# Building the gate matrix: the gating moved from GpSimd to ScalarE and VectorE, the loops written out

## The reference, cut to what matters

```python
best, ci = lax.top_k(cand, PEER_TOPK)
i1 = jnp.take_along_axis(top_i[..., 0, :], ci // PEER_TOPK, axis=-1)
i2 = jnp.take_along_axis(top_i[..., 1, :], ci % PEER_TOPK, axis=-1)
idx = i1 * PEER_N_KEYS + i2
g = jax.nn.softmax(best, axis=-1)
...
act = jax.nn.gelu(jnp.einsum('ckd,cd->ck', u_tab[ic], xc), approximate=False)
return jnp.einsum('ck,ckd->cd', (gc * act).astype(v_tab.dtype), v_tab[ic])
```

## Time and profile before

| | us |
|---|---|
| median of three timed runs | 2910.61 |
| lowest, highest of them | 2907.49, 2912.16 |
| the profiled execution's own time | 2909.95 |
| its span, first to last instruction | 2908.2 |
| VectorE busy | 2039.8 (70%) |
| TensorE matmul busy | 2516.1 (87%) |
| ScalarE busy | 1022.2 (35%) |
| GpSimd busy | 675.6 (23%) |

### The profile page before, as it was taken

One profiled execution on the slowest core, in us unless ns is written; L12 is line 12 of the kernel. 1 busy time (PEld: TensorE's weight loads), 2 busy tenths in 40 slices (PEclk: granted clock), 3 DMA queues, 4 the chain that ended last, 5 costly groups with the idle time before them and its releaser, 6 DMA issues. The chain is left out here.

```text
span 2908.2 us, 44667 instructions
## 1 busy us (share of the span) xinstructions
PE 2516.1 (87%) x15526; PEld 2263.0 (78%) x15528; DVE 2039.8 (70%) x3316; ACT 1022.2 (35%) x1576; POOL 675.6 (23%) x548
## 2 busy tenths in 40 slices
PE   7979267999999999888791679999999998768898
PEld 6758156999999999777581569999999997758797
DVE  7667999666666666586679996666666665649652
ACT  4321023444444444433210234444444443434321
POOL 5580265000000000046703650000000000616340
PEclk9879678999999999987796889999999999879898
DMA  5434000555555555453430015555555554324201
GB/s 191 145 116 147 20 0 29 189 187 188 188 187 188 187 186 186 133 182 130 135 133 8 0 42 189 188 188 187 188 187 186 185 186 144 117 102 145 66 1 37
DMA packets 107648, 392.09 MB, mean 135 GB/s; under 512 B 11952, under 2 KB 13360, under 8 KB 107184
## 3 DMA queue, kind: packets, MB, share of 16 engines
q1 hardware_dynamic: 107568, 391.02, 40.4%
HBM read 389.93 MB, written 1.05 MB: 134 GB/s over the span
## 5 line engine op out<-in xcount | busy, mean ns | idle before, releaser
L578 PEld LDWEIGHTS bank<-x_parts,chunk_parts 128*128 128x128 f32 x6144 | 770.5, 191 | 23.1 <-DVE chunk_parts L1126 3.5
L578 PE MATMUL bank<-x_parts,chunk_parts 128*128 128x256 f32 x6144 | 776.9, 283 | 2.5 <-DVE chunk_parts L1126 2.5
L1126 DVE TENSOR_TENSOR chunk_parts<-weight_ring,chunk_parts 128x1024 fp32r<-128x1024 f32 x512 | 625.3, 1222 | 195.6 <-ACT chunk_parts L762 195.6
L590 PE MATMUL bank<-chunk_parts,weight_parts 128*128 128x512 f32 x3072 | 744.8, 391 | 0.5 <-DVE chunk_parts L1126 0.5
L762 ACT CAST chunk_parts<-weight_ring 128x1024 fp32r<-128x1024 f32 x512 | 535.5, 1047 | 359.6 <-PE bank L590 359.6
L590 PEld LDWEIGHTS bank<-chunk_parts,weight_parts 128*128 128x128 f32 x3072 | 560.7, 188 | 106.8 <-issue 0.9
L1118 DVE TENSOR_TENSOR work<-work,big 128x256 f32<-128x256 f32 x256 | 162.9, 636 | 277.3 <-ACT work L766 277.3
L1094 DVE TENSOR_TENSOR weight_ring<-constants,work 128x512 f32<-128x512 f32 x256 | 262.3, 1100 | 4.1 <-ACT work L748 4.1
L766 ACT ACTIVATE work<-bank 128x256 f32<-128x256 f32 x256 | 98.3, 384 | 465.2 <-PE bank L578 465.2
L555 PE MATMUL bank<-weight_ring 128*128 128x128 f32 x1024 | 183.0, 335 | 83.9 <-issue 74.9
L555 PEld LDWEIGHTS bank<-weight_ring 128*128 128x128 f32 x1024 | 159.6, 238 | 107.7 <-issue 99.1
(11 more groups left out here) (355 smaller groups left out, 2788.7 us busy)
## 6 DMA issues: line engine op xcount, KB each, us to landing
weight_ring<-in_experts SPq DMA_DIRECT2D x512, 512.0 KB, 3.3
big<-in_ada SPq DMA_DIRECT2D x48, 512.0 KB, 4.0
weight_ring<-in_w_in SPq DMA_DIRECT2D x40, 512.0 KB, 4.6
weight_ring<-in_wq SPq DMA_DIRECT2D x32, 512.0 KB, 3.2
weight_ring<-in_gdn_in SPq DMA_DIRECT2D x32, 512.0 KB, 3.4
weight_ring<-in_w_out SPq DMA_DIRECT2D x16, 640.0 KB, 4.2
weight_ring<-in_lru_in SPq DMA_DIRECT2D x16, 512.0 KB, 3.3
weight_ring<-in_w_kv SPq DMA_DIRECT2D x8, 512.0 KB, 4.5
```

Of the source, the lines that this page charges most:

```text
L578: last = nc.tensor.matmul(nc_ps[2 + n % 2][:, 0:T], a[:, j * P:(j + 1) * P], xr[:, x, j], start=(j == 0 and a is hi and x == 0), stop=(j = ...
L590: last = nc.tensor.matmul(nc_ps[4 + 2 * tt + c][:, 0:512], wr[:, x, n % 2, tt * P:(tt + 1) * P], v[:, c * 512:(c + 1) * 512], start=False, ...
L1126: nc.vector.tensor_tensor(split[:, k % SPLITS, 1], wring[:, (N_ALL + k) % WSLOTS, 0:D], split[:, k % SPLITS, 0].bitcast(F32), ALU.subtract ...
```

## The change: what it does

- GpSimd's `gate_rows` and its loop are gone. GpSimd has nothing to do in the stage.
- VectorE compares only three of the four first one-hots (128 x 384, `first_hot`). The fourth it makes gated, in one instruction with two pointer scalars: equal to the key, then times the gate (128 x 128). The second one-hots stay as they were.
- ScalarE multiplies the three others by their gates, in place, with three 128 x 128 activations (Copy with a scale that is read from `slot`), one group ahead of its copy of the bank: the order on ScalarE is gate group g+1, copy group g.
- `ha` and `hb` are both rings of three groups (HOTS = 3), the PSUM banks stay two (G_BANKS = 2).
- On TensorE, ScalarE and VectorE the 64 groups are written out, with constant counts in place of registers; the semaphores start at zero.

```diff
+HOTS = 3
+ACT_GATED = 3
+G_BANKS = 2
...
-    ha = hot(4, 4, P)
-    hb = hot(2, 4, P)
+    ha = hot(HOTS, 4, P)
+    hb = hot(HOTS, 4, P)
...
-                        sp.wait_ge(s("g_ready"), 4 + GROUPS)
+                        sp.wait_ge(s("g_ready"), GROUPS)
...
-                def gate_products(g, count):
-                    pe.wait_ge(s("first_gated"), count)
-                    pe.wait_ge(s("second_hot"), count)
-                    pe.wait_ge(s("g_kept"), count)
+                for g in range(GROUPS):
+                    pe.wait_ge(s("first_gated"), g + 1)
+                    pe.wait_ge(s("second_hot"), g + 1)
+                    if g == 0:
+                        pe.wait_ge(s("slots_kept"), 1)
+                    if g >= G_BANKS:
+                        pe.wait_ge(s("g_kept"), g - G_BANKS + 1)
                     for j in range(4):
-                        last = nc.tensor.matmul(nc_ps[g % 2][:, j * P:(j + 1) * P], ha[:, g % 4, j], hb[:, g % 2, j], start=True, stop=True)
+                        last = nc.tensor.matmul(nc_ps[g % G_BANKS][:, j * P:(j + 1) * P], ha[:, g % HOTS, j], hb[:, g % HOTS, j], start=True, stop=True)
                     last.then_inc(s("g_ready"), 1)
-                with pe.Fori(0, GROUPS // ROUND) as i:
-                    for g in range(ROUND):
-                        gate_products(g, i * ROUND + (g + 1))
...
-                with act.Fori(0, T // 8) as i:
-                    for g in range(2):
-                        act.wait_ge(s("g_ready"), i * 2 + (g + 5))
-                        nc.scalar.copy(G[:, bass.ds(i * 8 + 4 * g, 4)], nc_ps[g][:, :].rearrange("p (a c) -> p a c", a=4)).then_inc(s("g_kept"), 1)
+                def gate_rows(g):
+                    act.wait_ge(s("first_hot"), g + 1)
+                    for j in range(ACT_GATED):
+                        last = nc.scalar.activation(ha[:, g % HOTS, j], ha[:, g % HOTS, j], ACT.Copy, scale=slot[:, 2, 4 * g + j:4 * g + j + 1])
+                    last.then_inc(s("first_gated"), 1)
+                gate_rows(0)
+                for g in range(GROUPS):
+                    if g + 1 < GROUPS:
+                        gate_rows(g + 1)
+                    act.wait_ge(s("g_ready"), g + 1)
+                    nc.scalar.copy(G[:, 4 * g:4 * g + 4], nc_ps[g % G_BANKS][:, :].rearrange("p (a c) -> p a c", a=4)).then_inc(s("g_kept"), 1)
...
-                def gate_rows(g, position, count):
-                    pool.wait_ge(s("first_hot"), count)
-                    nc.gpsimd.tensor_tensor(ha[:, g % 4], ha[:, g % 4], slot[:, 2, bass.ds(position, 4)].unsqueeze(2).broadcast_to([P, 4, P]),
-                                            ALU.mult).then_inc(s("first_gated"), 1)
...
-                def one_hot(out, half, position, ready):
-                    nc.vector.tensor_tensor(out, iota.unsqueeze(1).broadcast_to([P, 4, P]),
-                                            slot[:, half, bass.ds(position, 4)].unsqueeze(2).broadcast_to([P, 4, P]),
-                                            ALU.is_equal).then_inc(s(ready), 1)
...
+                def first_hot(g):
+                    if g >= HOTS:
+                        dve.wait_ge(s("g_ready"), g - HOTS + 1)
+                    n = ACT_GATED
+                    nc.vector.tensor_tensor(ha[:, g % HOTS, 0:n], iota.unsqueeze(1).broadcast_to([P, n, P]),
+                                            slot[:, 0, 4 * g:4 * g + n].unsqueeze(2).broadcast_to([P, n, P]), ALU.is_equal).then_inc(s("first_hot"), 1)
+                    for t in range(4 * g + n, 4 * g + 4):
+                        nc.vector.tensor_scalar(ha[:, g % HOTS, t % 4], iota, slot[:, 0, t:t + 1], slot[:, 2, t:t + 1], ALU.is_equal, ALU.mult)
+                first_hot(0)
+                for g in range(GROUPS):
                     if g + 1 < GROUPS:
-                        dve.wait_ge(s("g_ready"), g + 2)
-                        one_hot(ha[:, (g + 1) % 4], 0, 4 * (g + 1), "first_hot")
-                    dve.wait_ge(s("g_ready"), g + 3)
-                    one_hot(hb[:, g % 2], 1, 4 * g, "second_hot")
-                dve.wait_ge(s("g_kept"), 2 + T // 4)
+                        first_hot(g + 1)
+                    if g >= HOTS:
+                        dve.wait_ge(s("g_ready"), g - HOTS + 1)
+                    nc.vector.tensor_tensor(hb[:, g % HOTS], iota.unsqueeze(1).broadcast_to([P, 4, P]), slot[:, 1, 4 * g:4 * g + 4].unsqueeze(2).broadcast_to([P, 4, P]),
+                                            ALU.is_equal).then_inc(s("second_hot"), 1)
+                dve.wait_ge(s("g_kept"), GROUPS)
```

More of the change, by code:

```diff
@@ L223, in first_block @@
     hot.at = WSIZE + D
-    ha = hot(4, 4, P)
-    hb = hot(2, 4, P)
+    ha = hot(HOTS, 4, P)
+    hb = hot(HOTS, 4, P)
     GROUPS = T // 4
-    ROUND = 4
     out_e = big[:, 0:D]
@@ L546, in _ @@
                     last.then_inc(s("slots_turned"), 1)
-                def gate_products(g, count):
-                    pe.wait_ge(s("first_gated"), count)
-                    pe.wait_ge(s("second_hot"), count)
-                    pe.wait_ge(s("g_kept"), count)
+                for g in range(GROUPS):
[5 more added lines that the diff above has]
+                        pe.wait_ge(s("g_kept"), g - G_BANKS + 1)
                     for j in range(4):
-                        last = nc.tensor.matmul(nc_ps[g % 2][:, j * P:(j + 1) * P], ha[:, g % 4, j], hb[:, g % 2, j], start=True, stop=True)
+                        last = nc.tensor.matmul(nc_ps[g % G_BANKS][:, j * P:(j + 1) * P], ha[:, g % HOTS, j], hb[:, g % HOTS, j], start=True, stop=True)
                     last.then_inc(s("g_ready"), 1)
-                with pe.Fori(0, GROUPS // ROUND) as i:
-                    for g in range(ROUND):
-                        gate_products(g, i * ROUND + (g + 1))
-                pe.wait_ge(s("g_kept"), 2 + T // 4)
+                pe.wait_ge(s("g_kept"), GROUPS)
                 pe.wait_ge(s("zeros"), 1)
@@ L750, in _ @@
                 act.wait_ge(s("slots_kept"), 1)
-                act.sem_inc(s("g_kept"), 2)
-                with act.Fori(0, T // 8) as i:
-                    for g in range(2):
-                        act.wait_ge(s("g_ready"), i * 2 + (g + 5))
-                        nc.scalar.copy(G[:, bass.ds(i * 8 + 4 * g, 4)], nc_ps[g][:, :].rearrange("p (a c) -> p a c", a=4)).then_inc(s("g_kept"), 1)
+                def gate_rows(g):
[9 more added lines that the diff above has]
+                    nc.scalar.copy(G[:, 4 * g:4 * g + 4], nc_ps[g % G_BANKS][:, :].rearrange("p (a c) -> p a c", a=4)).then_inc(s("g_kept"), 1)
                 def high(k, slot_, loaded, free):
@@ L843, in _ @@
                                             ALU.mult).then_inc(s("hit_keyed"), 1)
-                def gate_rows(g, position, count):
-                    pool.wait_ge(s("first_hot"), count)
-                    nc.gpsimd.tensor_tensor(ha[:, g % 4], ha[:, g % 4], slot[:, 2, bass.ds(position, 4)].unsqueeze(2).broadcast_to([P, 4, P]),
-                                            ALU.mult).then_inc(s("first_gated"), 1)
-                with pool.Fori(0, GROUPS // ROUND) as i:
-                    for g in range(ROUND):
-                        gate_rows(g, i * (4 * ROUND) + 4 * g, i * ROUND + (g + 1))
             @block.vector
@@ L1090, in _ @@
                 dve.wait_ge(s("w_used"), N_ALL)
-                def one_hot(out, half, position, ready):
-                    nc.vector.tensor_tensor(out, iota.unsqueeze(1).broadcast_to([P, 4, P]),
-                                            slot[:, half, bass.ds(position, 4)].unsqueeze(2).broadcast_to([P, 4, P]),
-                                            ALU.is_equal).then_inc(s(ready), 1)
-                dve.sem_inc(s("g_ready"), 4)
-                one_hot(ha[:, 0], 0, 0, "first_hot")
@@ L1100, in _ @@
[L1100 to L1106, removed]
-                    if g + 1 < GROUPS:
-                        dve.wait_ge(s("g_ready"), g + 2)
-                        one_hot(ha[:, (g + 1) % 4], 0, 4 * (g + 1), "first_hot")
-                    dve.wait_ge(s("g_ready"), g + 3)
-                    one_hot(hb[:, g % 2], 1, 4 * g, "second_hot")
```

## The result

The changed kernel takes 2826.55 us (median of four runs, 2821.08 to 2828.64) against 2909.05 for the kernel before (median of four): 0.9715 of it, 95% interval 0.9694 to 0.9736. That is 82.5 us less, where 79 and 2831 were forecast. A second series of five runs beside the kernel before (after_again) gave 2821.83 us and 0.9701 (0.9684 to 0.9717).

What follows compares the result with a forecast made beforehand. VectorE, held by GpSimd, bounds the gate stage at 2.05 us a group; afterwards a circle of waits at 1.395. With start, end and clock terms the stage falls from 133.1 to 93.5 us, 79 in two layers: 2831 us, range 2820 to 2858.

Steps and rivals of the forecast that it cites:

- GpSimd's hold on VectorE: Gate stage: VectorE's two-input compares wait for GpSimd to finish; removing GpSimd saves 0.83 of 2.05 us a group.
- VectorE's own work: Gate stage: VectorE's three instructions a group without GpSimd, 0.49 + 0.20 + 0.61 = 1.30 us.
- The compare of 384 columns: VectorE's compare of three first one-hots: 560 ns, 0.49 us to the next start.
- The fourth one-hot: VectorE's gated 128 x 128 one-hot with two pointer scalars: 277 ns, 0.20 us as an interval.
- the bounds: Ends for unknown terms: fourth one-hot 0.14 to 0.40 us, with 0.26 between; gating 0.26 to 0.39.
- ScalarE's work: Gate stage: three gatings at 0.29 and a bank copy at 0.50 make 1.37 us a group.
- The circle: Gate stage: waits from TensorE to ScalarE's copy, gatings and back, 2.79 us per two groups, 1.395 each; the new bound.
- The clock: TensorE in the gate stage: full clock from a few groups on; 12% chance it goes on switching, 2842 us.
- Straight code at 0: Gate stage: writing the loops out gains nothing, as register instructions lay inside VectorE's 0.61 us; costed at 0.
- SP's wait: SP waits for the stage's last `g_ready`; its DMA comes as much earlier as the stage ends; costed at 0.
- the rings: Gate stage: the changed buffer rings, costed at 0 together with straight code and wait counts.
- the start counts: Gate stage: changed semaphore wait counts, costed at 0 together with straight code and rings.

Runs made afterwards that it cites:

- after_again: The changed kernel unaltered, run once more on one chip with its loop version: 2821.83 us, 0.9701 of the kernel before.
- pool_straight: Changed kernel's written-out code and rings of three, but GpSimd gates all four first one-hots and ScalarE only copies: 2908.28 us, 0.9999 of before.
- pool_beside: Changed kernel plus one GpSimd 128x512 multiply a group on an unused buffer, which nobody waits for inside the stage: 2953.54 us, 1.016 of before.
- act_less: Changed kernel without one of ScalarE's three gatings, so its result is not right: 2824.74 us, 0.9709 of before.
- both_less: Changed kernel without one ScalarE gating and VectorE's fourth one-hot, so its result is not right: 2806.81 us, 0.9643 of before.
- loops_again: Changed kernel with groups 4 to 63 in hardware loops on TensorE, ScalarE and VectorE, second run: 2834.6 us, 0.9738 of before.

## Why the prediction was right

*GpSimd's hold on VectorE, 0.83 us a group.* Right, and shown from both sides: pool_straight keeps it and stays at 2908 us, pool_beside brings it back without any wait, and the compares' 686 ns are the two free ones of the earlier trace rows.

*VectorE's own work, 1.30 us.* It is 0.47 + 0.26 + 0.615 = 1.345 by the starts in act_less. The compare of 384 columns was right (558 ns against 560). The fourth one-hot was under-sized, 342 ns against 277, because I read L1377's fastest time as one with two pointers. That line has the second pointer in only one of the two places where the kernel uses it; that this is why it was faster is argued, no run shows it. The row to take was L1840's 0.26, which stood in the bounds. It cost nothing, since ScalarE is 0.01 longer still.

*ScalarE's work, 1.37 us.* Right: 0.47 + 3 x 0.297 = 1.357, activations of 394 ns overlapping by 0.10.

*The circle, 1.395 us, as the bound.* The mechanism is there (both_less), but a term was over-sized: from TensorE's first matmul to the copy are 1.20 us, not 1.26. I had taken 1.26 from the earlier trace rows, where the copy runs in a hardware loop; the same stage written out, pool_straight, has 1.17 (its TensorE starts at 427.29, its copy at 428.46). With 1.20 the circle is (1.20 + 0.47 + 0.99 + 0.05) / 2 = 1.355, just level with ScalarE's queue, so what was named as the bound is one of two that tie. That is 0.04 us a group, 63 x 0.04 x 2 = 5 us, and about what lies between 2831 and 2826.55. The stage itself was forecast 2.7 us too long (93.5 against 90.8), which is 5 us in two layers as well.

*The clock.* Right. From 374 us the granted clock is 1.00 with TensorE busy for 68 of 80 us, and L1618 in the earlier trace rows was the proper row. The rule of the Trainium skill that I set against it ("TensorE: Matmul & The Clock Gate", on PSUM-queue cycling) doesn't describe this stage. The Trainium skill tells it there of a bf16 kernel with matmuls of 512 columns. This stage has float32 matmuls of 128, cycles through two banks with a gap of 0.20 us a group and does not swing. The kernel before (0.82) and pool_beside (0.66) do.

*Straight code at 0.* Right for the old kernel (pool_straight), wrong for the new one: written-out code is worth about 10 us once GpSimd no longer holds VectorE. As a forecast of the step it was wrong in form, since I costed the edit against a bound that another edit takes away. It did little harm to the sum, because the changed kernel is the written-out one and the rows for VectorE and ScalarE (1.30 and 1.37) came without loop ends. The one term with a loop in it was the 1.26.

*What was at 0 otherwise*: SP's wait, the rings, the start counts. The rings of three were run beside the old split only (pool_straight); what they are worth in the new one no run shows. SP's first DMA for the expert stage is issued at 453.84, with the last copy (453.66), as in the earlier trace rows, and the expert stage behind it has the same durations.

No kernel of the study beats the changed one with the whole work done.

## What to carry to other kernels

When an engine looks full, compare the durations of equal instructions: a factor of two between neighbours points to a hold, and what runs beside the long ones is the first suspect. Putting the suspect back as work that nobody waits for tests it. After a bound of this size falls, the next bounds can lie close together (here 1.357, 1.355 and 1.345 us a group), so costs that were free before, such as register arithmetic and loop ends, must be counted against the new pace. And a duration between two engines should be taken from a row whose instructions are addressed in the same way.

## What the runs showed of the hardware

- A GpSimd operation holds back a two-input VectorE compare that starts just behind it (by 0.10 and 0.12 us) until it has ended, whether it has two SBUF inputs (1.30 us, the compare grows by 1.06) or one (0.67 us, by 0.40), on buffers that have nothing to do with each other; the compare ends 0.53 to 0.55 us after GpSimd. A compare that was already running when GpSimd started kept its 0.68 us (pool_straight, 426.51). The Trainium skill ("GPSIMD Engine Reference", in the table of its section on specifications) says that GpSimd shares its SBUF interfaces with VectorE and that they contend when VectorE has two SBUF inputs. Both runs agree; that it is the interface to SBUF, and not something else that the two engines share, no run here separates.
- VectorE's one-tensor operation with two pointer scalars and 128 columns takes 342 ns and lets the next start after 0.26.
- Work on an otherwise idle GpSimd, though nobody waits for it, can cost time where VectorE is nearly full: 2827 us without, 2868 with a copy, 2954 with a multiply a group.
- Register addressing and loop ends cost nothing while another engine is the bound (pool_straight against the kernel before, 0.9999) and about 10 us where the queues are nearly full (loops_again against after_again).
